# Hybrid decoder layer on one core: the order of work in the attention loop, the first output tiles, the first up unit and the final norm

## The reference

```python
h = rms_norm(x) * (1.0 + scale1) + shift1
proj = h @ w_in[l]
q_a, k_a, v_a, q_g, k_g, v_g, g_out, z_lr = jnp.split(proj, SPLIT_POINTS, axis=-1)
attn = sliding_window_attention(q_a, k_a, v_a, attn_sinks[l], rel_bias)   # 8 heads, window 128
log_a = jax.nn.log_sigmoid(z_lr @ w_gate_up[l] + b_gate[l]) / GLA_GATE_NORM
o = rms_norm(gla_chunked(q_g, k_g, v_g, log_a)) * gla_norm_g[l]           # 4 heads, chunks of 64
gla = o * jax.nn.silu(g_out)
x = x + gate1 * (jnp.concatenate([attn, gla], axis=-1) @ w_out[l])
h = rms_norm(x) * (1.0 + scale2) + shift2
x = x + gate2 * (jnp.square(jax.nn.relu(h @ w_mlp_in[l])) @ w_mlp_out[l])
return rms_norm(x) * final_norm_g
```

## Time and profile before

| | before |
|---|---|
| three runs, us | 1053.34 to 1054.03, median 1053.83 |
| the profiled execution, us | 1053.77, of which its span is 1052.0 |
| TensorE busy | 1027.2 us, 98% of the span |
| VectorE, ScalarE, GpSimd busy | 708.1 us (67%), 474.6 us (45%), 95.6 us (9%) |
| mean granted TensorE clock | 0.998 of full speed |
| moved by DMA | 164.76 MB |

### The profile page before, as it was taken

How to read it: one execution, slowest core, us unless ns; L and a number is a source line. 1 busy time by engine, 2 the same in 40 slices (tenths; PEclk the granted TensorE clock), 3 DMA queues, 4 the chain that set the end, 5 groups by cost and what they waited for, 6 DMA issues and landing times.

```text
span 1052.0 us, 12967 instructions
## 1 busy us (share of the span) xinstructions
PE 1027.2 (98%) x5027; PEld 822.1 (78%) x5027; DVE 708.1 (67%) x926; ACT 474.6 (45%) x786; POOL 95.6 (9%) x123
## 2 busy tenths in 40 slices
PE   6999999999999999999999999999999999999997
PEld 4677887766676788878888888888888888888885
DVE  4576668788987364897556555553549963578886
ACT  7321012377776102775554544455453434335343
POOL 0111210022323000000000000000231000001100
PEclk9999999999999999999999999999999999999999
DMA  9977731200001713128345335327997332554633
GB/s 334 313 221 258 264 123 41 81 1 1 1 1 42 239 49 132 60 91 301 129 140 180 140 128 180 133 87 278 354 377 255 111 119 80 182 198 161 211 109 160
DMA packets 94052, 164.76 MB, mean 157 GB/s; under 512 B 15507, under 2 KB 44588, under 8 KB 93868
## 3 DMA queue, kind: packets, MB, share of 16 engines
q1 hardware_dynamic: 82108, 121.42, 34.3%
q0 software_dynamic: 11888, 42.55, 11.4%
HBM read 126.19 MB, written 39.33 MB: 157 GB/s over the span
## 4 chain that ended last, share of the span: by engine, by line
PE 55%; ACT 1%; DMA 1%; DVE 1%; issue 0%; SPq 0%; ACTq 0%
PE bank L1177 29%; PE bank L1158 26%; DMA dn_t<-in_w_mlp_out 1%; ACT h_hi_T L2201 0%; DVE h_T L1661 0%; ACT up_hi L2165 0%; ACT h_hi L2201 0%; DVE x L1863 0%; DVE up_lo L1617 0%; ACT hid_hi L2270 0%; ACT dn_hi L2273 0%; ACT hid L2233 0%; ACT out L2349 0%; DVE h L1648 0%; DVE x L1877 0%
## 5 line engine op out<-in xcount | busy, mean ns | idle before, releaser
L1177 PE MATMUL bank<-dn_hi,hid_hi 128*128 128x512 f32 x448 | 174.3, 389 | 0.0
L1177 PE MATMUL bank<-dn_lo,hid_hi 128*128 128x512 f32 x448 | 174.3, 389 | 0.0
L1177 PE MATMUL bank<-dn_hi,hid_lo 128*128 128x512 f32 x448 | 174.3, 389 | 0.0
L2270 ACT ACTIVATE hid_hi<-hid_raw 128x1024 fp32r<-128x1024 f32 x56 | 58.9, 1052 | 153.4 <-PE bank L1177 153.4
L1750 DVE TENSOR_TENSOR hid_lo<-hid_raw,hid_hi 128x1024 fp32r<-128x1024 f32 x56 | 68.3, 1220 | 84.7 <-ACT hid_hi L2270 84.7
L912 PE MATMUL bank<-w_hi,act_hi 128*128 128x512 f32 x252 | 101.5, 403 | 0.3
L1158 PE MATMUL bank<-h_hi_T,up_hi 128*128 128x512 f32 x256 | 99.9, 390 | 1.7 <-DVE h_lo_T L1657 1.3
L1617 DVE TENSOR_TENSOR up_lo<-up_raw,up_hi 128x1024 fp32r<-128x1024 f32 x48 | 58.7, 1223 | 61.1 <-ACT up_hi L2165 61.1
L1158 PE MATMUL bank<-h_hi_T,up_lo 128*128 128x512 f32 x256 | 99.6, 389 | 0.0
L1158 PE MATMUL bank<-h_lo_T,up_hi 128*128 128x512 f32 x256 | 99.6, 389 | 0.0
L912 PE MATMUL bank<-w_hi,act_lo 128*128 128x512 f32 x252 | 98.3, 390 | 0.0
(11 more groups left out here) (258 smaller groups left out, 1938.8 us busy)
## 6 DMA issues: line engine op xcount, KB each, us to landing
hidden_forms<-hid SPq DMA_DIRECT2D x56, 512.0 KB, 3.1
hid_raw<-hidden_forms SPq DMA_DIRECT2D x56, 512.0 KB, 3.9
ada_w<-in_w_ada POOLq DMA_DIRECT2D x32, 512.0 KB, 6.7
up_raw<-in_w_mlp_in SPq DMA_DIRECT2D x32, 512.0 KB, 5.5
dn_ring<-in_w_mlp_out POOLq DMA_DIRECT2D x24, 512.0 KB, 6.1
raw<-in_w_in SPq DMA_DIRECT2D x34, 256.0 KB, 4.7
ada_chunk<-in_w_ada SPq DMA_DIRECT2D x16, 512.0 KB, 8.6
dn_t<-in_w_mlp_out POOLq DMA_DIRECT2D x16, 512.0 KB, 8.0
```

Of the source, the lines that this page charges most:

```text
L1177: mm = pe.matmul(b, (hid_hi, hid_lo)[x][n % 2][:, k, t * P:(t + 1) * P], (dn_hi, dn_lo)[y][n % 2][:, k, :], start=(first and i == 0), stop ...
L2270: a.activation(hid_hi[n % 2][:, ks, :], hid_raw[n % 2][:, ks, :], ACT.Copy).then_inc(s_dhi, 1)
```

## The change

It changes the order of work in four places, and adds waits that the new order needs.

1. Attention loop. GpSimd's first SiLU instruction of block n waits until VectorE has normalised both head groups of block n (`s_pn`). `gla_next_state(n)` moves on VectorE from between the score read-outs of block n + 1 to behind `normalise(n, 1)`, and waits for linear attention's output of block n (`s_go_full`). `gla_scores(n)` moves on TensorE from inside the gate projection to between `probs_turned(n - 1, 1)` and `front(n, 1)`.
2. Output projection. On TensorE, the passes of tiles 1, 2 and 3 each move ahead of what they followed: tile 1 ahead of the transposes of group 0, tile 2 ahead of those of group 1, tile 3 ahead of `attend(7)`.
3. Up projection, unit 0. Products 2 to 6 run by a new function, `high_h_first`: for both banks first the matmuls that read the high part of h, then those that read its low part (`up_bank_ready` holds the waits for banks that stood in `up_product`). On VectorE and ScalarE the sums and splits of the forms change places.
4. Final norm. `upper_add(t + 1)` follows `one_newton(t)`, `one_var(t + 1)` follows `one_done(t)`, and ScalarE's logarithm takes the sum of squares itself, with the first half's share as its bias.

```diff
@@ -626,6 +626,7 @@
 
             for n in range(NT):
                 pool.wait_ge(s_g_copy, n + 1)
+                pool.wait_ge(s_pn, 2 * n + 2)
                 pool.tensor_scalar(g_low[:, :], g_copy[:, :], -1.0, 0.0, ALU.mult, ALU.max).then_inc(s_pool, 1)
                 pool.wait_ge(s_pool, n + 1)
                 pool.wait_ge(s_sg_e, n + 1)
@@ -1061,10 +1062,10 @@
                 probs_turned(n - 1, 0)
                 front(n, 0)
                 probs_turned(n - 1, 1)
+                gla_scores(n)
                 front(n, 1)
                 attend(n - 1)
                 g_out(n, 0)
-                gla_scores(n)
                 g_out(n, 1, range(0, 2))
                 out_turned(n - 1)
                 gla_keys(n)
@@ -1080,13 +1081,13 @@
 
             pe.wait_ge(s_sc_free, 4 * NT)
             high_first_pass(SLOT_O, 0, bank[O_BANK[0]][:, :])
+            out_pass(0, 0, 1)
             probs_turned(NT - 1, 0)
-            out_pass(0, 0, 1)
-            probs_turned(NT - 1, 1)
             pe.wait_ge(s_st_b, NT)
             out_pass(0, 0, 2)
+            probs_turned(NT - 1, 1)
+            out_pass(0, 0, 3)
             attend(NT - 1)
-            out_pass(0, 0, 3)
             out_turned(NT - 1)
             out_pass(0, 0, 4)
             out_pass(0, 0, 5)
@@ -1161,8 +1165,39 @@
                         n += 1
                 mm.then_inc(s_prod, 1)
 
+            def high_h_first(i):
+
+                name = UP_H[i]
+
+                def one(x, y, k, m, start, stop):
+                    return pe.matmul(bank[UP_BANKS[i][m]][:, :], (up_hi, up_lo)[x][i % 4][:, k, m * P:(m + 1) * P],
+                                     (h_hi, h_lo)[y][name][:, k, :], start=start, stop=stop, skip_group_check=True)
+
+                for m in range(2):
+                    if m == 0:
+                        pe.wait_ge(s_whi, i + 1)
+                    up_bank_ready(0, i, m)
+                    for j in range(2):
+                        if m == 0:
+                            pe.wait_ge(s_hhi, 2 * H_HI_ORDER.index(name) + j + 1)
+                        for k in range(2 * j, 2 * j + 2):
+                            one(0, 0, k, m, UP_STARTS[i] and k == 0, False)
+                        if m == 0 and j == 0:
+                            pe.wait_ge(s_wlo, i + 1)
+                        for k in range(2 * j, 2 * j + 2):
+                            one(1, 0, k, m, False, False)
+                for m in range(2):
+                    for k in range(4):
+                        if m == 0 and k % 2 == 0:
+                            pe.wait_ge(s_hlo, 2 * H_ORDER.index(name) + k // 2 + 1)
+                        mm = one(0, 1, k, m, False, k == 3)
+                    mm.then_inc(s_prod, 1)
+
             for u in range(NU):
                 for i in range(NP):
+                    if u == 0 and i >= 2:
+                        high_h_first(i)
+                        continue
                     for m in range(2):
                         up_product(u, i, m)
                         if u == 0 and (i, m) in ((UP_P1, 1), (UP_P2, 0)):
@@ -1536,6 +1571,7 @@
             def gla_next_state(n):
 
                 v.wait_ge(s_st_b, n + 1)
+                v.wait_ge(s_go_full, n + 1)
                 for tt in range(2):
                     ins = v.scalar_tensor_tensor(state_a[:, tt, :], state_b[:, tt, :], dec(n, 1, tt),
                                                  bank[7][:, tt * P:(tt + 1) * P], ALU.mult, ALU.add)
@@ -1565,12 +1601,12 @@
             gla_state_b(0)
             normalise(0, 0)
             normalise(0, 1)
+            gla_next_state(0)
             LINKS = 12
 
             def block(n):
                 scores(n, 0)
                 gla_variance(n - 1)
-                gla_next_state(n - 1)
                 scores(n, 1)
                 gla_finish(n - 1)
                 v.wait_ge(s_at_full, n + 1)
@@ -1584,6 +1620,7 @@
                 normalise(n, 0)
                 gla_state_b(n)
                 normalise(n, 1)
+                gla_next_state(n)
                 own.leave(NT - 2)
             block(NT - 1)
             gla_state_b(NT - 1)
@@ -1700,16 +1737,16 @@
             v.wait_ge(*h_ready(1, 3))
             form_sum("T1", "12", "11")
             wide_lo(2)
-            form_lo("T1")
             v.wait_ge(s_x1_out[1], 64)
             affine(1, 7)
-            wide_lo(3)
             v.wait_ge(*h_ready(1, 6))
             v.wait_ge(*h_ready(1, 7))
             v.wait_ge(s_hsum, 1)
             form_sum("T2", "22", "T1")
+            form_lo("T1")
+            wide_lo(3)
+            form_sum("T3", "22", "12")
             form_lo("T2")
-            form_sum("T3", "22", "12")
 
             def up_add(u, dst, bank_of, ready, i, done):
                 for m in range(2):
@@ -1765,9 +1802,9 @@
                     wide_lo(f + 6)
                 else:
                     wide_lo(4)
+                    v.wait_ge(s_hlo, 2 * (H_ORDER.index("T2") + 1))
+                    form_sum("T4", "21", "T2")
                     form_lo("T3")
-                    v.wait_ge(s_hsum, 2)
-                    form_sum("T4", "21", "T2")
                     wide_lo(5)
                     form_lo("T4")
                     up_add(u, HID_22, Z_UP, s_u3, UP_P5, s_c22)
@@ -1833,9 +1870,9 @@
 
                 cols = slice(4, NT)
                 v.wait_ge(s_sq, SQ_FIRST + 3)
+                own.link(v.tensor_scalar(ssq_first[:, 0:4], ssq_first[:, 0:4], 1.0 / D, EPS, ALU.mult, ALU.add))
                 own.link(v.tensor_tensor(var[:, cols], ssq_first[:, cols], ssq[:, cols], ALU.add))
                 v.tensor_scalar(var[:, cols], var[:, cols], 1.0 / D, EPS, ALU.mult, ALU.add).then_inc(s_var, 1)
-                own.link(v.tensor_scalar(ssq_first[:, 0:4], ssq_first[:, 0:4], 1.0 / D, EPS, ALU.mult, ALU.add))
                 v.wait_ge(s_var, ROOT_FIRST + 1)
                 v.wait_ge(s_root, ROOT_FIRST + 1)
                 own.link(newton(rstd[:, cols], var[:, cols], newt[:, cols]))
@@ -1851,6 +1888,7 @@
             def one_newton(t):
 
                 c = slice(t, t + 1)
+                v.wait_ge(s_var, ROOT_FIRST + 1 + t + 1)
                 v.wait_ge(s_root, ROOT_FIRST + 1 + t + 1)
                 own.link(v.scalar_tensor_tensor(newt[:, c], rstd[:, c], rstd[:, c], var[:, c], ALU.mult, ALU.mult))
                 own.link(v.tensor_scalar(newt[:, c], newt[:, c], -0.5, 1.5, ALU.mult, ALU.add))
@@ -1925,12 +1963,12 @@
             upper_add(0)
             one_var(0)
             for t in range(4):
+                one_newton(t)
                 if t < 3:
                     upper_add(t + 1)
-                one_newton(t)
+                one_done(t)
                 if t < 3:
                     one_var(t + 1)
-                one_done(t)
 
 
         @block.scalar
@@ -2186,10 +2224,12 @@
                              bias=ada_col[:, 3 * KT + k:3 * KT + k + 1], scale=ada_col[:, 4 * KT + k:4 * KT + k + 1])\
                     .then_inc(s_aff_s, 1)
 
-            def form_hi(name):
+            def form_hi(name, between=None):
 
                 for j in range(2):
                     ks = slice(2 * j, 2 * j + 2)
+                    if j == 1 and between is not None:
+                        between()
                     if name in ("11", "21", "22"):
                         half, k = int(name[1]) - 1, 4 * (int(name[0]) - 1) + 2 * j
                         a.wait_ge(*h_ready(half, k))
@@ -2197,7 +2237,7 @@
                     else:
                         a.wait_ge(s_hsum, int(name[1]))
                     if name == "T4":
-                        a.wait_ge(s_hlo, 2 * (H_ORDER.index("T3") + 1))
+                        a.wait_ge(s_hlo, 2 * H_ORDER.index("T3") + j + 1)
                     a.activation(h_hi[name][:, ks, :], h_full[name][:, ks, :], ACT.Copy).then_inc(s_hhi, 1)
 
             wide_hi(0)
@@ -2219,11 +2259,11 @@
             affine(1, 0)
             affine(1, 2)
             wide_hi(2)
-            wide_hi(3)
-            form_hi("T1")
             a.wait_ge(s_x1_out[1], 64)
             for k in (4, 5, 6):
                 affine(1, k)
+            form_hi("T1")
+            wide_hi(3)
 
             def kept(dst, u, m, i, done):
 
@@ -2308,9 +2348,8 @@
                     for m in range(2):
                         kept(HID_S3, u, m, UP_P6, s_u2)
                     wide_hi(6)
-                    form_hi("T4")
-                    for m in range(2):
-                        kept(HID_22, u, m, UP_P7, s_u3)
+                    form_hi("T4", between=lambda: kept(HID_22, u, 0, UP_P7, s_u3))
+                    kept(HID_22, u, 1, UP_P7, s_u3)
                     wide_hi(7)
                     relu_21(u)
                     relu_squared(HID_11, u, s_c11)
@@ -2374,6 +2413,13 @@
                     final_squares((6, 7), 0, out_u2, ssq, 6).then_inc(s_sq, 1)
                     final_root(slice(4, NT), 1)
 
+            def one_root(t):
+
+                c = slice(t, t + 1)
```

(6 more changed lines are left out.)

14 lines of the change are left out of this document (8 added, 6 removed).

## The result

The changed kernel takes 1043.62 us (median of 4 runs, 1043.39 to 1043.80) beside 1053.89 us for the kernel before on the same chip: a ratio of 0.9904, 95% interval 0.9890 to 0.9919, or 10.3 us won. The profiled execution's span fell from 1052.0 to 1041.9 us, and the granted clock is 0.998 after.

The account below looks back on a forecast made before the run. TensorE, busy 98% of the span, bounds the kernel, so only its gaps can be won. 4.6 + 1.75 - 0.15 + 1.6 + 0.3 = 8.1 us off 1053.77 gives 1045.7 us, range 1044.6 to 1048.7.

Parts of the forecast that it names:

- What bounds the kernel, and which waits go: Whole kernel: TensorE, busy 98%, bounds; waits on normalised probabilities (3.1 us) and scores' read-out (1.5 us) can be won.
- the slack that was read for it: Attention loop: GpSimd's SiLU chain may come 1.4 us later before TensorE feels it; then each us costs one per block.
- The loop: Attention loop: 0.7 us saved in five blocks, 0.5 in block 1, 0.6 in block 7; 4.6 us in all.
- the price of linear attention's place inside the gate projection: Attention loop, gate projection: linear attention's scores standing inside it cost TensorE 0.74 us a block.
- Why group 1's normalising took 2.58 us: Attention loop, VectorE: GpSimd's first SiLU instruction running beside it adds 1.44 us to the 1.14 us needed.
- Output projection: Output projection's first tiles: a tile pass covers the transposes' wait, 1.75 us won, less 0.15 us for w_out's second slot.
- the second slot: Output projection: w_out's second weight slot keeps 0.6 us of slack; cost between 0 and 1.5 us, taken as 0.15.
- First up unit: Up projection, unit 0: high part of h first removes waits on low parts; 1.6 us won after hand-off costs.
- hand-offs: First up unit: both banks finish 0.9 us apart, ScalarE must copy the first within that; 0.1 us cost.
- Final norm: Final norm, last tile: ScalarE's logarithm no longer waits 0.28 us for VectorE's variance; 0.3 us won.
- The first rival: First up unit and w_out's second slot: stalls only move, worth 1.6 to 2.3 us, 1047.3 to 1048.0 us; chance 0.14.
- The third rival: Attention loop: GpSimd isn't what slows the normalising; loop saves 1.4 us, total 4.9 us, 1048.9 us; chance 0.04.

Follow-up runs that it names:

- first experiment: The kernel before with one line added: GpSimd waits until VectorE has normalised group 1; 1051.83 us beside 1053.59, ratio 0.9982.
- third experiments: The changed kernel without GpSimd's wait for the normalising of group 1; 1046.23 us, 2.6 us slower, ratio to the kernel before 0.9929.

## Where the prediction was right, and the step that failed

The time lies 1.0 us below the range. The mechanism held in all four places, and sizes were off: 1.3 of the 2.1 us are in the loop's term, and 0.9 us of those in one price.

- **What bounds the kernel, and which waits go:** right. Each wait named is gone, TensorE stays the bound, and the tail of the loop's GpSimd chain had the slack that was read for it.
- **The loop, 4.6 us forecast, 5.9 measured: the term that failed.** The step is the price of linear attention's place inside the gate projection, "0.97 us apart, where two of them alone are 0.23 us apart". I priced the place from the two starts around it. But the matmul after such a switch delays its successor too: starts 0.31 to 0.34 us apart in place of 0.23. The matmul behind that of 309.08 in block 6 before:

```profile
309.42 0.39 PE L912 MATMUL bank<-w_lo,act_hi 128*128 128x512 f32 x1
```

  From 309.08 to 309.42 it is 0.34 us. Measured over the whole projection the place costs 0.86 us, 0.12 us more in each of 7 blocks, or 0.9 us. A further 0.27 us is block 1, for which I took 0.5 us and which gained 0.89: its front part takes as long before and after (6.60 and 6.63 us), so it gains the place like every other block. Rounding 0.73 down to 0.7 in five blocks made up 0.15 us.
- **Why group 1's normalising took 2.58 us: right about GpSimd, wrong about which instruction.** I laid the 1.44 us to GpSimd's first instruction alone. 1.08 us of it stand beside its second, the add (first experiment). The sum didn't depend on it, since the new wait holds both back.
- **Output projection, 1.6 us forecast, 1.96 measured.** The 1.75 us were right in size, though two parts of the change each give them. Two things were missed: one tile pass fewer is entered from small matmuls (the three passes beside them take 8.49 us in place of 8.65), and the second slot cost nothing in this execution, where I had taken 0.15. It came close: VectorE's split ends at 349.22 + 2.35 = 351.57 and the first matmul that needs it starts at 351.80, so 0.2 us of the forecast 0.6 us of slack is left. From the end of attention's matmuls to the split's start it is 8.8 us (340.40 to 349.22), where it was 8.4.

```profile
349.22 2.35 DVE L1638 SCALAR_TENSOR_TENSOR w_lo<-raw,small,w_hi 128x2048 fp32r<-128x2048 f32 x1 [6.78 <-ACT w_hi L2185]
```

- **First up unit, 1.6 us forecast, 2.0 measured.** A third gap of 0.14 us and the slow start behind each gap (3 x 0.08 us) were left out; the 0.1 us for hand-offs came as 0.15.
- **Final norm, 0.3 us forecast, 0.17 measured.** The 0.13 us at the end of the up units lie within what that wait differs between executions: luck, not forecast and not the change.
- **The range.** Its lower end was built from the forecast's own terms with all costs at zero, so it shared their common error: every price of a switch was read from two neighbouring starts. An end made of the sum's own terms doesn't cover a mistake in how they are read.
- **The rivals.** The Trainium skill, "SBUF — State Buffer", section "Who interferes with whom", would have the moved GpSimd pair undisturbed, since VectorE reads a bank and one tile beside it: the trace agrees (1.92 and 1.27 us). Of the same section's lock, under which whoever comes second is held for the whole instruction, the trace bears out a part: VectorE's fourth multiplication is held to the end of GpSimd's add (301.16 against 301.01), but two others ran at full speed inside GpSimd's first instruction. The first rival stood at the door: the second slot has 0.2 us left, and an execution with the same loop (the unit undone) waited for it and lost 0.45 us. The third rival, that GpSimd isn't the cause, is ruled out by the first and third experiments.

## What to carry to other kernels

Price the place of a piece of work from the whole stretch that it interrupts, with it and without it, and not from the two starts beside it; small float32 matmuls are cheapest next to others like them. Removing a wait on the bounding engine pays only if the next thing it needs is ready or other work is put in the gap: here GpSimd's wait alone gave the loop nothing, and the order without it 3.5 of 5.9 us. When two edits cure the same wait, only undoing one and doing one alone shows it.
